# Making most of layer 0's modulation rows inside the first mixer instead of ahead of it

## The reference, cut to what matters

```python
silu_c, silu_cc = silu(c), silu(c_ctx)
for layer in range(2):
    mod_lat = silu_c @ ada_w[layer] + ada_b[layer]        # 1024 x 6144
    mod_ctx = silu_cc @ ada_w[layer] + ada_b[layer]
    sh1, sc1, g1, sh2, sc2, g2 = split(mod_lat, 6)         # the same for context
    a = rmsnorm(h, mix_norm_g) * (1 + sc1) + sh1
    h = h + g1 * mixer(a)            # layer 0: retention and short convolution, layer 1: attention
    f = rmsnorm(h, ffn_norm_g) * (1 + sc2) + sh2
    h = h + g2 * peer_ffn(f)
out = rmsnorm(h_lat, final_norm_g)
```

## Time and profile before

| | us |
|---|---|
| median of 3 runs | 4231.73 (4230.95 to 4233.16) |
| the profiled execution | 4230.58 |
| its span in the trace | 4228.8 |
| first stage | 0 to 84.0 |
| mixer 0, up to the load of the strips | 84.0 to 312.6 |
| retention part | 312.6 to 425.3 |

### The profile page before, as it was taken

One profiled execution on the slowest core, in us unless ns is written; L12 is line 12 of the kernel. 1 busy time (PEld: TensorE's weight loads), 2 busy tenths in 40 slices (PEclk: granted clock), 3 DMA queues, 4 the chain that ended last, 5 costly groups with the idle time before them and its releaser, 6 DMA issues. The chain is left out here.

```text
span 4228.8 us, 33315 instructions
## 1 busy us (share of the span) xinstructions
PE 3457.1 (82%) x10024; PEld 1626.7 (38%) x10024; DVE 2684.6 (63%) x6235; ACT 1563.9 (37%) x4522; POOL 1544.0 (37%) x1350
## 2 busy tenths in 40 slices
PE   4999877788887788788777769997877977977786
PEld 0894632333333233233222237884322322322222
DVE  3314398857857857866864445656887587587454
ACT  3210143343343343343333333542434434433333
POOL 1004044444444444444444420002444454444442
PEclk7998999999999999999999988998999999999999
DMA  8127299999999999999999951006999999999998
GB/s 351 50 73 267 95 399 400 421 421 422 418 421 419 413 418 419 414 416 419 415 414 421 422 199 48 1 11 257 399 421 421 421 415 419 421 416 413 421 421 331
DMA packets 215396, 1455.27 MB, mean 344 GB/s; under 512 B 25920, under 2 KB 25920, under 8 KB 44080
## 3 DMA queue, kind: packets, MB, share of 16 engines
q0 software_dynamic: 184704, 1342.31, 76.7%
q1 hardware_dynamic: 30400, 110.72, 7.0%
q10 hardware_dynamic: 112, 0.11, 0.0%
HBM read 1447.72 MB, written 5.34 MB: 344 GB/s over the span
## 5 line engine op out<-in xcount | busy, mean ns | idle before, releaser
L1419 PE MATMUL peer_py<-peer_ring,peer_diag 128*128 128x512 f32 x5120 | 2507.9, 625 | 620.5 <-ACT peer_diag L1349 609.9
L1519 DVE CUSTOM_DVE_ANT_0 peer_ring<-peer_ring,peer_f 128x1024 f32<-128x1024 f32 x1280 | 1556.2, 1225 | 921.3 <-DMA peer_ring<-in_uv_dram,peer_idx 912.7
L1302 POOL DMA_INDIRECT peer_ring<-in_uv_dram,peer_idx x1280 | 1454.5, 1136 | 1817.8 <-PE peer_py L1419 1687.4
L1419 PEld LDWEIGHTS peer_py<-peer_ring,peer_diag 128*128 128x128 f32 x5120 | 928.3, 194 | 2152.3 <-ACT peer_diag L1349 1323.9
L1343 ACT ACTIVATE peer_gel<-peer_u 128x1 f32<-128x1 f32 x1280 | 258.8, 202 | 1830.2 <-DVE peer_u L1519 1828.7
L1349 ACT ACTIVATE peer_diag<-ident,peer_coef 128x128 f32<-128x128 f32 x1280 | 513.8, 401 | 41.7
L1347 ACT ACTIVATE peer_coef<-peer_gel,peer_gate 128x1 f32<-128x1 f32 x1280 | 377.1, 295 | 46.4
L353 DVE TENSOR_TENSOR m_w_low<-m_w_low_plain,m_w_high 128x2048 fp32r<-128x2048 f32 x26 | 61.1, 2348 | 219.3 <-ACT m_w_high L348 219.2
L361 PE MATMUL m_ps<-m_w_high,m_aT_high 128*128 128x512 f32 x416 | 165.7, 398 | 3.6 <-DVE m_v L820 1.9
L1394 PE MATMUL peer_pb<-arena,peer_fT 128*128 128x512 f32 x320 | 164.7, 612 | 2.4 <-ACT peer_fT L1316 2.4
L1293 POOL IOTA peer_iota<- 128x16 f32 x2 | 0.3, 144 | 452.1 <-POOLq L836 364.3
(11 more groups left out here) (193 smaller groups left out, 2594.8 us busy)
## 6 DMA issues: line engine op xcount, KB each, us to landing
mod_rows_sb<-in_ada_w_dram SPq DMA_DIRECT2D x33, 1024.0 KB, 5.0
peer_ring<-in_uv_dram,peer_idx POOLq DMA_INDIRECT x1280, 15.0
arena<-in_ada_w_dram SPq DMA_DIRECT2D x15, 1024.0 KB, 16.2
m_w_low_plain<-in_ev_w_in_dram SPq DMA_DIRECT2D x12, 1024.0 KB, 5.0
arena<-in_peer_wq_dram SPq DMA_DIRECT2D x2, 4096.0 KB, 18.4
mod_rows_sb<-mod_rows SPq DMA_DIRECT2D x7, 1024.0 KB, 7.0
m_w_low_plain<-in_od_w_in_dram SPq DMA_DIRECT2D x6, 1024.0 KB, 5.3
m_w_low_plain<-in_ev_w_out_dram SPq DMA_DIRECT2D x4, 1024.0 KB, 5.0
```

The costliest lines, as they stand in the source:

```text
L1302: pool.indirect_dma_start(ring[:, n % RING], None, A["uv"], bass.IndirectOffsetOnAxis(idx[:, i % 2, hd, k:k + 1], 0)).then_inc(sem(f"lande ...
L1419: ins = pe.matmul(PY[:, i % 2, b], diag[:, n % RING], ring[:, n % RING, D + b * HALF:D + (b + 1) * HALF], start=s == 0, stop=s == TS - 1)
L1519: dve.tensor_tensor_reduce(x, x, f[:, i % 2], 1.0, 0.0, ALU.mult, ALU.add, u[:, n % RING:n % RING + 1]).then_inc(sem("dot"), 1)
```

## The change

The first stage makes group 0 of layer 0 alone (`FRONT`). The other two groups of layer 0 and the three of layer 1 (`LATE`, 5 groups, 40 pieces) are made in the retention part of mixer 0, in the same two buffers. Items 3 to 14 do two pieces each, items 15 to 30 one each (`late_pieces`). The terms of layer 1 reuse the space of layer 0's, so SP loads them in the middle, ahead of piece 22, when the rows of the second late group are made. The stores go from POOL to ScalarE, each behind a part of a head (`STORE_AFTER`). VectorE has one row buffer for all five groups and waits for the store of the one before. The gate rows of mixer 0 are loaded behind the last piece, and the residual at the stage's end waits for them. All the arithmetic is the same.

```diff
+FRONT = (0,)
+LATE = ((0, 1), (0, 2), (1, 0), (1, 1), (1, 2))
+N_LATE = len(LATE) * KC
+DOUBLE_FROM, DOUBLE_TO = 3, 15
+def late_pieces(i):
+    if i < DOUBLE_FROM:
+        return range(0)
+    if i < DOUBLE_TO:
+        return range(2 * (i - DOUBLE_FROM), 2 * (i - DOUBLE_FROM) + 2)
+    n = 2 * (DOUBLE_TO - DOUBLE_FROM) + i - DOUBLE_TO
+    return range(n, min(n + 1, N_LATE))
...
-            for n in range(GROUPS * KC):
+            for n in range(len(FRONT) * KC):
...
-            load_group_terms(act, A, 0, bias, gain, S("terms_loaded"))
+            load_group_terms(act, A, 0, FRONT, bias, gain, S("terms_loaded"))
...
-            for g in range(GROUPS):
+            for g in FRONT:
...
-                    load_group_terms(sp, A, 1, mod1_bias, mod1_gain, S("mod1_terms"))
+                    load_group_terms(sp, A, 0, (1, 2), late_bias, late_gain, S("late_terms"))
                     sp.wait_ge(S("m0_a"), NT)
-                    for n in range(GROUPS * KC):
+                    for n in range(N_LATE):
                         if n >= 2:
-                            sp.wait_ge(S("mod1_mm"), n - 1)
-                        load_piece(sp, A, 1, n // KC, n % KC, pieces[n % 2]).then_inc(S(f"mod1_piece{n % 2}"), 16)
-                    sp.wait_ge(S("mod1_rows"), GROUPS)
+                            sp.wait_ge(S("late_mm"), n - 1)
+                        if n == 3 * KC - 2:
+                            sp.wait_ge(S("late_rows"), 2)
+                            load_group_terms(sp, A, 1, range(GROUPS), late_bias, late_gain, S("late_terms"))
+                        layer, g = LATE[n // KC]
+                        load_piece(sp, A, layer, g, n % KC, pieces[n % 2]).then_inc(S(f"late_piece{n % 2}"), 16)
+                    sp.wait_ge(S("late_stored"), 16 * 2 * TILES)
+                    load_rows(sp, S, mod_d, rows, 0, 0, "m0_gates", parts=slice(2, 3))
+                    sp.wait_ge(S("late_rows"), len(LATE))
...
-                    load_rows(sp, S, mod_d, rows, 0, 0, "m0_tabs", parts=slice(2, 3))
...
-            for g in range(GROUPS):
-                pool.wait_ge(S("mod1_rows"), g + 1)
-                store_group(pool, mod_d, 1, g, mod1_row, S("mod1_stored"))
...
+                if g in STORE_AFTER:
+                    late = STORE_AFTER.index(g)
+                    act.wait_ge(S("late_rows"), late + 1)
+                    store_group(act, mod_d, *LATE[late], late_row, S("late_stored"))
...
-                if 0 <= i - FIRST_PIECE < GROUPS * KC:
-                    modulation(i - FIRST_PIECE)
+                for n in late_pieces(i):
+                    modulation(n)
```

More of the change, by code:

```diff
@@ L96, in load_piece, with terms_count, load_group_terms @@
     return sp.dma_start(piece, A["ada_w"][layer].rearrange("(p k) n -> p k n", p=P)[:, k, g * GROUP:(g + 1) * GROUP])
-def load_group_terms(sp, A, layer, bias, gain, sem):
-    for g in range(GROUPS):
+FRONT = (0,)
[9 more added lines that the diff above has]
+    return range(n, min(n + 1, N_LATE))
+def terms_count(groups):
+    return 16 * sum(1 + (group_tile(g, j)[1] == 1) for g in groups for j in range(TILES))
+def load_group_terms(sp, A, layer, groups, bias, gain, sem):
+    for g in groups:
         for j in range(TILES):
@@ L245, in _ @@
                 dve.tensor_tensor(strips[:, hd, 0:SL], dec[:, 0], dec[:, 1], ALU.add).then_inc(S("strip"), 1)
-            dve.wait_ge(S("terms_loaded"), 16 * GROUP_TERMS)
+            dve.wait_ge(S("terms_loaded"), terms_count(FRONT))
             done = 0
-            for g in range(GROUPS):
+            for g in FRONT:
                 dve.wait_ge(S("mod_mm"), KC * (g + 1))
@@ L476, in mixer0_stage @@
         terms = wl[0][:, 1].rearrange("p k n -> p (k n)").rearrange("p (g n) -> p g n", g=GROUPS + 1)
-        mod1_bias, mod1_gain = terms[:, 0:GROUPS], terms[:, GROUPS]
-        mod1_row = tables[:].rearrange("p a t n -> p (a t n)")
-        FIRST_PIECE = 3
+        late_bias, late_gain = terms[:, 0:GROUPS], terms[:, GROUPS]
+        late_row = tables[:].rearrange("p a t n -> p (a t n)")
+        STORE_AFTER = (0, 1, 2, 4, 6)
         norm_pairs = (6, 4, 6, 4, 6, 6)
@@ L528, in _ @@
                     sp.dma_start(cw[:], A["conv_wT"].rearrange("(m p) i -> p m i", p=P)).then_inc(S("m0_tabs"), 16)
[L529 removed]
             load_peer()
+            sp.wait_ge(S("late_stored"), 16 * len(LATE) * TILES)
         @block.gpsimd
@@ L534, in _ @@
             norm_shift(pool, S, T, a, rows)
-            pool.wait_ge(S("m0_tabs"), 80)
+            pool.wait_ge(S("m0_tabs"), 48)
             pool.wait_ge(S("m0_u"), n_ch)
@@ L697, in modulation @@
                 g, k = divmod(n, KC)
-                pe.wait_ge(S(f"mod1_piece{n % 2}"), 16 * (n // 2 + 1))
+                pe.wait_ge(S(f"late_piece{n % 2}"), 16 * (n // 2 + 1))
                 if k == 0 and g >= 2:
-                    pe.wait_ge(S("mod1_rows"), g - 1)
-                group_sums(pe, PS[:, g % 2], silu, pieces[n % 2], k).then_inc(S("mod1_mm"), 1)
+                    pe.wait_ge(S("late_rows"), g - 1)
+                group_sums(pe, PS[:, g % 2], silu, pieces[n % 2], k).then_inc(S("late_mm"), 1)
             for i in range(len(items)):
@@ L740, in _ @@
             split_low(dve, S, T, wh, wl, 2)
-            dve.wait_ge(S("m0_tabs"), 80)
+            dve.wait_ge(S("m0_tabs"), 48)
             dve.wait_ge(S("m0_aT_ps"), NT)
@@ L785, in head_norm @@
                 ins.then_inc(S("m0_ret_y"), 1)
-            mod1_done = 0
+            late_done = 0
             for i, (hd, kd, j) in enumerate(items):
@@ L807, in _ @@
                     head_norm(hd, 0)
[L808 to L815, removed]
+                for n in late_pieces(i - 1):
+                    late, k = divmod(n, KC)
+                    if k < KC - 1:
+                        continue
+                    layer, g = LATE[late]
+                    dve.wait_ge(S("late_terms"), terms_count((1, 2)) + (terms_count(range(GROUPS)) if layer else 0))
+                    if late:
+                        dve.wait_ge(S("late_stored"), 16 * TILES * late)
+                    dve.wait_ge(S("late_mm"), n + 1)
+                    late_done = group_rows(dve, S, "late", g, late_row, PS[:, late % 2], late_bias, late_gain, late_done)
             head_norm(RET_HEADS - 1, 1)
@@ L827, in _ @@
             dve.wait_ge(S("m0_pv"), len(items))
+            dve.wait_ge(S("m0_gates"), 32)
             residual(dve, S, T, h, PS, rows, PT, list(range(NT)), lambda n: n % 8, lambda: split_low(dve, S, T, wh, wl, 2 * n_in + 3))
@@ L886, in _ @@
         def _(sp):
-            sp.wait_ge(S("mod1_stored"), 16 * GROUPS * TILES)
+            sp.wait_ge(S("late_stored"), 16 * len(LATE) * TILES)
             load_rows(sp, S, mod_d, rows, 1, 0, "m1_rows", parts=slice(0, 2))
```

6 lines of the change are left out of this document (2 added, 4 removed).

## The result

| | before | after |
|---|---|---|
| median of the runs, us | 4231.3 | 4262.8 (4256.0 to 4269.7) |
| profiled execution / its span | 4230.6 / 4228.8 | 4264.1 / 4262.2 |
| mixer 0 starts | 84.00 | 61.07 |
| load of the strips | 312.61 | 290.82 |
| transposes (end of the retention part) | 425.25 | 461.64 |

The ratio after to before is 1.0075, 95% interval 1.0057 to 1.0092: slower by 31.5 us at the medians, against 27.2 forecast (4257.8, range 4243 to 4272). In the two traces the 33.4 us are: first stage -22.9, mixer 0 up to the strips +1.1, retention part 170.8 instead of 112.6, +58.2, everything behind it -3.0. The program behind it is the same, and what made the 3.0 is open.

The account below looks back on a forecast made before the run. Transfers, then the strips' chain, bound the first stage; a saturated two-buffer ring replaces TensorE in the double items. First stage -21.3 plus retention part +48.5 gave +27.2 on 4230.6: 4257.8 us, range 4243 to 4272.

Parts of the forecast that it names:

- First stage: Before mixer 0: with 8 pieces loaded instead of 24, the decay strips' chain bounds it; mixer starts at 62.7, -21.3 us.
- Start of the part: Retention part's beginning: piece 0 there at 327.43 as before, clock back in item 4's pieces, item 5's pieces begin at 342.3.
- Items 5 to 14: Double items in the retention part: two-buffer ring bounds at 6.1 us an item, nine steps 54.9; two clock falls add 4.
- the rival of half the clock throughout: Double items of the retention part: half clock holds through them, clock term 14 instead of 4, total 4268; chance 0.17.
- The stall of the small loads: Ahead of piece 22: SP issues layer 1's 16 small loads, 5.2 us as before, with nothing seen that hides it.
- Single items: Items 15 to 30: fifteen steps of 3.11 us and about 1 until the clock is back; last piece's matmuls end at 459.5.
- The end: Item 31 to transposes: scores, strip product, last group's rows, four ScalarE stores ahead of its last Square, together 10.3 us.
- The rival of the data rate: Retention part: two loads in flight hide latency, pieces come every 2.49 us, total 4235.7, no measurable change; chance 0.09.

## Why the prediction was right, point by point

- **First stage, -21.3: measured -22.9.** The chain of the strips was the next bound, as said. The store landed in 8.6 us, not 10.2: the reading back, taken as the nearest row, is the slower one. It was issued 0.4 earlier, and 0.5 was lost between landing and mixer.
- **Start of the part, 14.9 us from piece 0 to item 5: 15.4** (304.19 to 319.57). Piece 0's matmuls began 13.4 after the load of the strips instead of the 14.8 of before: six small loads were gone that I had at nothing, and SP issued the piece 4.1 after the strips instead of 6.1.
- **Items 5 to 14, 54.9 and 4 for the clock: 67.2** beside the stall. This is the term that was mis-sized. That the ring can do 6.1 the run with two filler matmuls bears out (6.09). What I had at 4 for the clock was 12 for the clock and late landings together: I had a gap of 1.45 between an item's two pieces, but where the clock fell in this stretch TensorE had waited 2.6 to 3.1 us, or 1.66 close behind 2.32. Where both loads of an item had left within 2 us of each other, the second landed 6.7 to 7.4 after its issue. And I counted two falls of the clock where it fell four times in nine items. The measured 4262.8 lies between the forecast and the rival of half the clock throughout (4268); the truth is a change between the two, with a mean granted clock of 0.69. The Trainium skill's "TensorE: Matmul & The Clock Gate", section "HAM oscillation", describes this: bursts of matmuls between waits for DMA, each starting cold. The trace agrees in part: the row at 330.14 runs at half the clock behind a wait of 2.71 us, but not each burst starts cold, as the row at 326.39 behind a wait of 0.89 us runs at the full one.
- **The stall of the small loads, 5.3: 5.2** from the matmuls of piece 20 to the issue of piece 22 (381.98 to 387.15), and 8.3 us on to piece 24 (391.95 to 400.25) as walked.
- **Single items, 48.7 to the end of the last piece: 50.9**, fifteen steps of 3.32 rather than 3.11 and 1 for the clock; two late loads cost the clock once more at 431.
- **The end, 10.3: 10.5.** The group's rows (452.86 to 457.11), ScalarE's stores (457.20 to 458.35) and only then the last Square.
- **The rival of the data rate** (4235.7, "no measurable change") did not come true. The run with four buffers came out near its price, 4231.5, but partly by chance: its pieces took 103 us from the first to the last and not 114, and 18.8 us without pieces followed, not 10.3.
- **What lay outside the sum.** The retention part was 9.7 us longer than forecast (170.8 against 161.2). In the traces the first stage gave 1.6 more than forecast and everything behind the part 3.0, which I had at nothing, against 1.1 more ahead of the strips. That the median is only 5 us off is in part luck.

So the order of the bounds was as forecast: strips, ring, stall, rows at the end. In the double items the ring was not the bound throughout but took turns with a TensorE at half the clock, and the size that was off was the price of that.

## What to carry to other kernels

Moving transfers out of a stage that waits for them saves only down to that stage's next bound (23 us here, where 16 MB at 410 GB/s are 41, an estimate), while the stage that receives them pays their full time once its own slack is used; compare both before moving everything, and move only as much as the first stage can't hide beside its next bound (eight pieces less, with four buffers, gave a ratio of 0.9966 instead of 0.9999). Ask of every ring how long a buffer takes from free to free: at two deep it was about 6.1 us for two pieces that the data rate brings in 5.3, and TensorE, which waited 2 to 3 us for them, lost its clock on top. Put loads of another kind on a queue where no refill waits behind them.

## What was not expected of the hardware

- Adding 1.85 us of useless matmuls to each of twelve items made nine of them 12.7 us shorter (59.7 against 72.4 us), with TensorE's granted clock at 1.00 where it had been 0.69. The median went from 4262.8 to 4254.3, with intervals that overlap.
- The granted clock fell in or right behind waits of 2.6 to 3.1 us in the changed kernel, and once in one of 1.66 close behind one of 2.32.
- A store of 3 MB from SBUF landed in 8.6 us in the changed kernel; the same bytes took 10.2 to come back in the kernel before, with other loads issued behind them.
- POOL needed 0.52 us to issue one of the small loads, SP 0.24 to 0.32.
